# A two-block kernel on one core: filler matmuls in TensorE's waits, all PSUM banks open, and the pooled branch in another order

## The chip, the cores and the metric

The kernel runs on one core of one Trainium2 chip. The metric is the device time of one execution in microseconds (us). The core's engines run side by side: TensorE (PE, matrix products), VectorE (DVE), ScalarE (ACT, which also issues some DMAs), GpSimd (POOL), and SyncE (SP, here only DMAs). They meet through semaphores. All data is float32.

## The reference, cut to what matters

```python
def first_block(x, c, ...):            # x: 512 tokens x 1024
    shift1, scale1, gate1, shift2, scale2, gate2 = split(silu(c) @ w_ada + b_ada)
    a = rms(x, norm1_w) * (1 + scale1) + shift1
    x = x + gate1 * hybrid_mixer(a)    # SSD + dilated attention + pooling, summed, @ w_out
    a = rms(x, norm2_w) * (1 + scale2) + shift2
    return x + gate2 * (relu(a @ w_ff1) ** 2 @ w_ff2)

def second_block(x, c, ctx, c_ctx, ...):   # 512 latent and 256 context tokens, 4 layers
    for i, mixer in enumerate((window_gqa, mla, mlstm, window_gqa)):
        sh, sc, gt = split(silu(c) @ w_ada_i + b_ada_i)      # the same for c_ctx
        h = rms(x, g_pre_i) * (1 + sc) + sh                  # latent and context
        x = x + gt * rms(mixer(h), g_post_i)
    return x_lat
```

The pooled branch of the hybrid mixer takes `u = a @ w_in[u]` in four groups of 256 channels, subtracts from group g its causal mean over 2, 4, 8 or 16 tokens, mixes each group with a 256x256 matrix, scales, and gives `sigmoid(a @ w_in[g_pool]) * (mixed @ w_pool_out)` to the sum of the branches.

## The kernel before, in words

**Layout.** Activations lie feature-major: a tensor of 1024 features is 8 chunks of 128 partitions by the tokens. Each operand of a large product is split into a rounded part and a remainder (`a_hi`, `a_lo`; `w_hi`, `w_lo`), and `products` (L414 to L418) makes three matmuls of each pair of chunks. A tile of 128 outputs by 512 tokens over 8 chunks is 24 matmuls into one PSUM bank.

**Weights.** They arrive in 156 slots of 128x2048 in a ring of three. SP starts the DMA of a slot when the slot three earlier is used up, ACT writes `w_hi` (L411), POOL writes `w_lo` in four pieces (L402), and PE waits for `lo_ready`. A slot holds two full tiles. The order of the slots is fixed by `slot_plan` (L49).

**`dense`** (L421) is the stage that nearly all large products go through. It takes named weight sections, a function that gives a slot's tiles, and what ACT (`act_tile`), DVE (`dve_tile`) and ACT again (`act_last`) do to each finished tile. PE takes a bank only when the tile `ring` places back has been read out; `ring` is 4 where a slot has at most two tiles, else 6 or 8. In all stages ACT starts with a wait until every tile of the stages before has been read out (L497 ff.), DVE too. With `lead=2` the first two tiles run side by side, chunk by chunk, as the chunks of `a` come. `rhs_ready` holds what PE waits for before a chunk that another engine still has to write.

**Modulation.** The six and twelve vectors `silu(c) @ w_ada` are worked out on DVE: 72 slots are streamed in, and one slot is two instructions of 128x1024 (L765), or four from slot 24 on, where both conditioning vectors are needed. The slots are shared out over the tiles of some `dense` stages: in group form 8 in the setup, 8 in `z`, 8 in the SSD's output stage, 16 in `qkv0` and `qkv1` (8 each), 32 in the eight feed-forward stages (4 each). A slot's products stand on DVE ahead of the work on that tile.

**Order of the program.** First norm (L967), SSD branch (`z`, `dt`, `xbc`, then small stages of transposes, states and heads, L1140 to L1340), its norm (`rms_scale`, L827) and output; dilated attention (`qkv0` to `qkv3` with `HeadNorms` L1409 as side work, then the last norms alone, then `group_attention` L1475); output of it; the pooled branch (L2036); `out`; a norm (`pre_norm`, L866); four pairs of feed-forward stages `ff1_b`, `ff2_b` (L2163 to L2182). Then the second block: A0 (window attention, L1726), B (latent attention, `pair_attention`, L1578), C (mLSTM) and A3 (window attention again), each with its `pre_norm`, where PE sums squares into all rows with a matrix of ones (L913).

**The pooled branch before.** `u` runs through groups 0 to 3 (2-wide mean first); ACT copies each tile, and `pool_tile` on DVE takes the mean by doublings (L2069) and splits the result into `m_hi`, `m_lo` (group 3 needs the most instructions). `mix` waits for them and `scaled` (L2097) makes `x_hi`, `x_lo`. `gated` (L1342) then runs four turns of two gate tiles (`g_pool`, a product with `a`) and two output tiles (`pool_out`, a product with `x`). Its `dense` starts once all of `mix` is read out, since ACT's entry wait and the bank ring both ask for it.

**The attention stages.** `window_attention` issues the scores of pair p+1, transposes and value products of earlier pairs; `pair_attention` does the same with three banks of 512 a score. In B, `finish_both` (on DVE, L2375, L599, L600) multiplies a head pair's output with its gate over all 768 tokens when its last query block is done, and the output stage waits for that.

## Time and profile before

| | |
|---|---|
| median of 3 runs | 3040.9 us |
| lowest and highest | 3038.96, 3047.11 us |
| the profiled execution | 3038.86 us |
| its span in the trace | 3037.1 us |
| mean granted TensorE clock | 0.965 of full |
| PE busy | 2781.2 us (92%) |
| DVE busy | 1629.8 us (54%) |
| ACT busy | 1224.1 us (40%) |
| POOL busy | 955.4 us (31%) |

The span is what the instructions take on the device; the execution's own time has 1.8 us more around it. Busy PE time counts overlapping records once. Two records of one float32 matmul stand in the trace, one of each product matmul of `dense`. The granted clock of TensorE has two levels here, full (2.4 GHz, shown as 1.0) and half (1.2 GHz).

### The profile page before, as it was taken

How to read it: one execution, taken by the hardware profiler on the slowest of the kernel's cores; microseconds unless marked ns; L12 is line 12 of the kernel's file. 1: busy time of each engine (PE TensorE's matmuls, PEld its weight loads, DVE VectorE, ACT ScalarE, POOL GpSimd, SP SyncE). 2: the span in 40 equal slices, each digit the busy share in tenths (PEclk: the TensorE clock that was granted, in tenths of full speed). 3: DMA queues.
4: the chain of work that ended last, by engine and by line, in shares of the span. 5: the costliest groups of instructions: out<-in, count | busy, mean ns of one | idle time of the engine just before them, and what ended most of it. 6: DMA issues, size and time to landing. Idle time of an engine off the chain costs nothing.

```text
span 3037.1 us, 39956 instructions
## 1 busy us (share of the span) xinstructions
PE 2781.2 (92%) x16048; PEld 2289.2 (75%) x16048; DVE 1629.8 (54%) x3096; ACT 1224.1 (40%) x2113; POOL 955.4 (31%) x636
## 2 busy tenths in 40 slices
PE   5978989889899899989999989999899999889996
PEld 4746878678687788869876868677689998768785
DVE  6686394162832999960288341354490238551583
ACT  4334234543123222242278354543442326353582
POOL 4612475304453666633300213100233220113301
PEclk8989999999999999999999999999999999999998
DMA  8303562202323555521200221101122331122201
GB/s 322 123 28 146 189 219 104 98 1 84 125 96 126 194 193 182 194 112 69 95 10 2 84 83 56 42 1 49 61 85 69 140 131 51 56 83 102 72 2 70
DMA packets 52329, 300.07 MB, mean 99 GB/s; under 512 B 4592, under 2 KB 5936, under 8 KB 22320
## 3 DMA queue, kind: packets, MB, share of 16 engines
q1 hardware_dynamic: 22464, 163.59, 15.2%
q10 hardware_dynamic: 29680, 133.92, 11.7%
q8 instruction: 128, 2.10, 0.3%
q14 instruction: 57, 0.47, 0.0%
HBM read 271.25 MB, written 21.00 MB: 96 GB/s over the span
## 4 chain that ended last, share of the span: by engine, by line
PE 67%; DVE 14%; ACT 4%; issue 2%; DMA 0%; ACTq 0%; DVEq 0%
PE psum L416 17%; PE psum L417 17%; PE psum L418 17%; DVE ada_temp L765 4%; PE psum L1768 2%; PE psum L913 2%; PE psum L1610 2%; PE psum L3054 2%; PE psum L1633 2%; PE psum L1789 2%; DVE pair_row L1818 1%; PE psum L1778 1%; PE psum L1614 1%; PE psum L1622 1%; DVE pair_prob L1827 1%
## 5 line engine op out<-in xcount | busy, mean ns | idle before, releaser
L402 POOL TENSOR_TENSOR w_lo<-raw,w_hi 128x512 fp32r<-128x512 f32 x624 | 945.3, 1546 | 2039.9 <-ACT w_hi L411 2039.8
L416 PE MATMUL psum<-a_hi,w_hi 128*128 128x512 f32 (+2 forms) x1880 | 709.1, 377 | 71.9 <-DVE a_lo L922 20.6
L418 PE MATMUL psum<-a_hi,w_lo 128*128 128x512 f32 (+2 forms) x1880 | 698.7, 372 | 0.0
L417 PE MATMUL psum<-a_lo,w_hi 128*128 128x512 f32 (+2 forms) x1880 | 698.6, 372 | 0.0
L416 PEld LDWEIGHTS psum<-a_hi,w_hi 128*128 128x128 f32 (+1 forms) x1880 | 358.1, 190 | 147.4 <-issue 44.4
L765 DVE SCALAR_TENSOR_TENSOR ada_temp<-ada_ring,ada_rows 128x1024 f32<-128x1024 f32 x224 | 393.1, 1810 | 48.5 <-ACT ada_rows L725 21.3
L417 PEld LDWEIGHTS psum<-a_lo,w_hi 128*128 128x128 f32 (+1 forms) x1880 | 358.3, 191 | 64.0 <-issue 3.6
L418 PEld LDWEIGHTS psum<-a_hi,w_lo 128*128 128x128 f32 (+1 forms) x1880 | 357.0, 190 | 62.8
L411 ACT ACTIVATE w_hi<-raw 128x2048 fp32r<-128x2048 f32 x156 | 298.2, 1912 | 243.9 <-DMA raw<-stream 133.5
L416 PE MATMUL psum<-w_hi,a_hi 128*128 128x256 f32 x800 | 229.7, 287 | 1.1 <-POOL w_lo L402 0.6
L417 PE MATMUL psum<-w_lo,a_hi 128*128 128x256 f32 x800 | 226.3, 283 | 0.0
L418 PE MATMUL psum<-w_hi,a_lo 128*128 128x256 f32 x800 | 226.3, 283 | 0.0
L416 PEld LDWEIGHTS psum<-w_hi,a_hi 128*128 128x128 f32 x800 | 153.4, 192 | 3.4 <-issue 1.4
L417 PEld LDWEIGHTS psum<-w_lo,a_hi 128*128 128x128 f32 x800 | 153.5, 192 | 1.4 <-issue 1.4
L418 PEld LDWEIGHTS psum<-w_hi,a_lo 128*128 128x128 f32 x800 | 153.4, 192 | 0.0
L1818 DVE CUSTOM_DVE_ANT_0 pair_row<-psum,pair_mask,neg_sinks 128x512 f32<-128x512 f32 (+2 forms) x160 | 116.6, 747 | 37.7 <-PE psum L1768 24.8
L1846 ACT ACTIVATE pair_prob<-pair_row,pair_stat 128x513 f32<-128x513 f32 (+2 forms) x160 | 114.8, 719 | 42.3 <-DVE pair_stat L1818 24.8
L2308 DVE TENSOR_TENSOR square<-y 128x512 f32<-128x512 f32 (+1 forms) x56 | 33.3, 594 | 173.8 <-ACT y L2314 173.8
L1768 PE MATMUL psum<-gk,gq 64*128 64x128 f32 (+1 forms) x960 | 97.7, 338 | 17.3 <-DVE pair_stat L1818 15.5
L2314 ACT ACTIVATE y<-psum 128x512 f32<-128x512 f32 (+1 forms) x56 | 28.3, 506 | 199.2 <-PE psum L418 198.8
L416 PE MATMUL psum<-hid_hi,w_hi 128*128 128x512 f32 x256 | 99.8, 390 | 1.4 <-DVE hid_lo L600 1.4
L1768 PEld LDWEIGHTS psum<-gk,gq 64*128 64x128 f32 x960 | 72.0, 194 | 36.7 <-DVE pair_stat L1818 23.4
(397 smaller groups left out, 4633.3 us busy)
## 6 DMA issues: line engine op xcount, KB each, us to landing
raw<-stream SPq DMA_DIRECT2D x156, 1024.0 KB, 4.8
ada_ring<-ada ACTq DMA_DIRECT2D x72, 1024.0 KB, 5.7
xres<-x_in ACTq DMA_DIRECT2D x4, 3072.0 KB, 11.1
x_in<-xres ACTq DMA_DIRECT2D x3, 3072.0 KB, 10.8
gates<-gate_part ACTq DMA_DIRECT2D x8, 768.0 KB, 4.2
partner<-gq ACTq DMA_DIRECT2D x4, 1024.0 KB, 10.2
c_rows_m<-rows_m ACTq DMA_DIRECT2D x2, 1536.0 KB, 9.3
c_og<-gates ACTq DMA_DIRECT2D x4, 768.0 KB, 5.7
```

Source lines behind the costliest of these rows:

```text
L402: last = pool.tensor_tensor(k.w_lo[:, r, cols], k.raw[:, r, cols], k.w_hi[:, r, cols].bitcast(F32), ALU.subtract)
L411: act.activation(k.w_hi[:, r], k.raw[:, r], ACT.Copy).then_inc(k.hi_ready, 1)
L416: pe.matmul(out, lhs[0], rhs[0], start=start, stop=False)
L417: pe.matmul(out, lhs[0], rhs[1], start=False, stop=False)
L418: return pe.matmul(out, lhs[1], rhs[0], start=False, stop=stop)
L765: dve.scalar_tensor_tensor(self.temp[:, self.products % 2], self.ring[:, place, c], 1.0, self.used_rows[:, w], ALU.mult, ALU.mult, accum_o ...
L913: pe.matmul(k.psum[:, banks[n], 0:t1 - t0], k.cst("ones"), squares[:, i % 2, 0:t1 - t0], start=c == 0, stop=c == KC - 1).then_inc(summed.s ...
L1610: pe.matmul(score(u)[:, col:col + cols], q, keys, start=True, stop=False)
L1633: last = pe.matmul(value_bank(u), units[u]["pv"][j], prob_t[:, u % n_t, j * P:(j + 1) * P], start=j == 0, stop=j == n_blocks - 1)
L1768: last = pe.matmul(score(u)[:, col:col + cols], q, keys, start=True, stop=True)
L1818: dve.tensor_tensor_reduce(row[:, u % 4, 1:1 + w], score(u), mask[:, un["mask"]:un["mask"] + w], 1.0, un["sink"], ALU.add, ALU.min, stat[: ...
L1846: act.activation(prob[:, u % 4, 0:1 + width(u)], row[:, u % 4, 0:1 + width(u)], ACT.Exp, bias=stat[:, 0, u % 4:u % 4 + 1], scale=-1.0, acc ...
```

## The change

- **Fillers.** `keep_busy(pe, bank, n)` issues n float32 matmuls (a 128x128 matrix of ones by 256 constant columns) into a bank that nobody reads. They stand in PE's program ahead of a wait or behind one: in `z` ahead of chunk 4 (4) and chunk 6 (14); after `xbc` (11); in the SSD's small stages (2, 8, 5, 7); in `rms_scale` (5, it is called with two groups); around the last head norms (6 and 11); at the start of `ff1_0` (10) and `ff2_0` (4); in `pre_norm` of the second block ahead of the latent and the context sums (6 and 6; in A0 only the second); at the start of `Aq`, `Bin` and `Cqk` (5 each); in window attention behind the scores in turns 0 and 1 (5 each) and at its end (4); at the end of B's attention (11); in C ahead of the last head's first turn (20) and at its end (4).
- **Banks.** `ring` is now every bank a stage may use (8, or 6 where `n_banks=6`).
- **ScalarE's entry.** With `untaken=n`, ACT's wait at the start of a stage allows n tiles of the stages before to be still unread, and where the stage has no `act_tile` it doesn't wait at all. `ff1_1` to `ff1_3`, `ff2_b` and the pooled stages use `untaken=8`.
- **Pooled branch.** `u` and `mix` go through the groups from 3 to 0; a stage `g_pool0` (the gate tiles of turn 0, kept in `sig`, now four tiles) stands between them; then three turns each have the gates of the next turn and the output tiles of this one; `pool_out3` is last.
- **Modulation.** The dilated attention's group shrinks from 16 slots to 12 (`qkv1` 8 to 4), the feed-forward's grows from 32 to 36 (each `ff1_b` 4 to 3, each `ff2_b` 4 to 6).
- **B's gate product** is made in two parts: latent tokens after query block 3, context tokens after block 5.

```diff
-    slots("u", "w_in", full, R(u0, 1024))
-    slots("mix", "mix", (0, 1024), R(0, 256))
+    slots("u", "w_in", full, [x for g in (3, 2, 1, 0) for x in R(u0 + 256 * g, 256)])
     for c in range(4):
         slots(f"g_pool{c}", "w_in", full, R(g0 + 2048 + 256 * c, 256))
-        slots(f"pool_out{c}", "w_pool_out", full, R(256 * c, 256))
+        if c:
+            slots(f"pool_out{c - 1}", "w_pool_out", full, R(256 * c - 256, 256))
+        else:
+            slots("mix", "mix", (0, 1024), R(0, 256))
+    slots("pool_out3", "w_pool_out", full, R(768, 256))
...
+    def keep_busy(self, pe, bank, n):
+        for _ in range(n):
+            pe.matmul(bank[:, 0:256], self.cst("ones"), self.const[:, 0:256], start=True, stop=True)
...
-    ring = 4 if max(per) <= 2 else 6 if max(per) % 3 == 0 else 8
...
-    ring = min(ring, n_banks - k.odd_banks)
+    ring = n_banks - k.odd_banks
...
                     pe.wait_ge(free.sem, free.at(together - ring))
+                    k.keep_busy(pe, bank(0), fill)
                     for j in range(len(slot_tiles[0][1])):
+                        if lead_fill and j in lead_fill:
+                            pe.wait_ge(free.sem, free.at(together + 1 - ring))
+                            k.keep_busy(pe, bank(together), lead_fill[j])
...
                     pe.wait_ge(free.sem, free.at(t + 1 - ring))
+                    if t == 0:
+                        k.keep_busy(pe, bank(t), fill)
...
-        act.wait_ge(free.sem, free.at(0))
+        if act_tile is not None or untaken == 0:
+            act.wait_ge(free.sem, free.at(-untaken))
...
+    if fill_end:
+        @block.tensor
+        def _(pe):
+            pe.wait_ge(free.sem, free.at(1 - n_banks))
+            k.keep_busy(pe, bank(total), fill_end)
...
+            if c == 0 and fill[n]:
+                pe.wait_ge(k.tile_free.sem, k.tile_free.at(0))
+                k.keep_busy(pe, k.psum[:, next(b for b in (2, 3, 4) if b not in banks), :], fill[n])
             pe.wait_ge(sq.sem, sq.at(i + 1))
...
+        pe.wait_ge(masked.sem, masked.at(2 * n))
+        k.keep_busy(pe, k.psum[:, 0, :], 11)
...
             if p + 1 < n:
                 scores(p + 1)
+            if p < 2:
+                k.keep_busy(pe, k.psum[:, 7, :], 5)
             if p >= 3:
                 values(p - 3)
+        pe.wait_ge(masked.sem, masked.at(2 * n))
+        k.keep_busy(pe, k.psum[:, 0, :], 4)
...
-    ada = k.ada.group(16, B0 + 36864, B0 + 61440, rest + 20480, 3, new_rows=True)
+    ada = k.ada.group(12, B0 + 36864, B0 + 61440, rest + 20480, 3, new_rows=True)
...
+    pooled = k.free_of
+    sig = k.at("sig", B0 + 100352, [P, 4, S])
+    dense(k, block, ["g_pool0"], feature_major(a, KC, [(0, S)]), barrier=False, untaken=KC,
+          dve_tile=lambda dve, i, t, ps: dve.nop(),
+          act_tile=lambda act, i, t, ps: act.activation(sig[:, t, :], ps, ACT.Sigmoid))
...
+    k.rhs_ready = {(j, 2 * g + c): (k.tile_free.sem, pooled[2 * g + j])
                    for g in range(4) for c in range(2) for j in range(2)}
-    dense(k, block, ["mix"], mix_tiles, dve_tile=scaled, barrier=False)
+    dense(k, block, ["mix"], mix_tiles, dve_tile=scaled, barrier=False, untaken=KC)
...
+    def gate_ahead(act, i, t, ps):
+        if t >= 2:
+            act.wait_ge(k.staged.sem, staged + 4 * i + t)
+            return act.nop()
+        if i:
+            act.wait_ge(k.tile_free.sem, start + 4 * i - 1 + t)
+        return act.activation(sig[:, 2 * ((i + 1) % 2) + t, :], ps, ACT.Sigmoid)
...
+    k.rhs_ready = {(j, 2): (k.tile_free.sem, mixed_at[j]) for j in range(KC)}
+    dense(k, block, [f"{x_}" for c in range(3) for x_ in (f"g_pool{c + 1}", f"pool_out{c}")],
+          lambda s, hi, lo: feature_major(x if s else a, KC, [(0, S)])(s, hi, lo), turn_slots=2, act_tile=gate_ahead,
+          dve_tile=project, barrier=False, untaken=KC)
...
+    dense(k, block, ["pool_out3"], feature_major(x, KC, [(0, S)]), barrier=False, untaken=KC,
+          dve_tile=lambda dve, i, t, ps: add_chunk(dve, 6 + t, ps))
...
-    ada = k.ada.group(32, B0 + 57344, A0 + 40960, B0 + 81920, 3, new_rows=True)
+    ada = k.ada.group(36, B0 + 57344, A0 + 40960, B0 + 81920, 3, new_rows=True)
...
-              ada=ada.of(4), barrier=False)
+              ada=ada.of(3), barrier=False, untaken=KC if b else 0)
...
-        dense(k, block, [f"ff2_{b}"], feature_major(hid, KC, full), dve_tile=add_ff, ada=ada.of(4), barrier=False)
+        dense(k, block, [f"ff2_{b}"], feature_major(hid, KC, full), dve_tile=add_ff, ada=ada.of(6), barrier=False, fill=0 if b else 4, untaken=KC)
...
-        if b == 5:
-            pair["finish"] = finish_both(c)
+        if b in (3, 5):
+            pair["finish"] = finish_both(c, LAT if b == 3 else CTX)
...
+                if (h, c) == (H - 1, 0):
+                    k.keep_busy(pe, front(q), 20)
                 pe.wait_ge(normed.sem, normed.at(6 * h + 6))
```

**What it moves on ScalarE, pooled branch.** `u` is the copy of a tile of `u`, `sig` a gate tile, `w_hi` a weight slot's rounding, `x_in` the residual read back; the stage borders are the branches. Before:

```order
L2080 ACTIVATE u_6340<-psum 128x512
L496 UNCONDITIONAL_BRANCH
L411 ACTIVATE w_hi_51<-raw_49 128x2048
L2105 UNCONDITIONAL_BRANCH
L2139 DMA x_in_6339<-xT 128x8x512
L2140 DMA x_in_6339<-ctxT 128x8x256
L496 UNCONDITIONAL_BRANCH
L1356 ACTIVATE sig_6864<-psum 128x512
```

And of the change:

```order
L2126 ACTIVATE u_6373<-psum 128x512
L514 UNCONDITIONAL_BRANCH
L2133 ACTIVATE sig_6756<-psum 128x512
L421 ACTIVATE w_hi_51<-raw_49 128x2048
L2133 ACTIVATE sig_6756<-psum 128x512
L514 UNCONDITIONAL_BRANCH
L421 ACTIVATE w_hi_51<-raw_49 128x2048
L2157 UNCONDITIONAL_BRANCH
L2221 DMA x_in_6372<-xT 128x8x512
L2222 DMA x_in_6372<-ctxT 128x8x256
L514 UNCONDITIONAL_BRANCH
L2173 ACTIVATE sig_6756<-psum 128x512
```

The first two gate tiles and one more weight slot now stand between the last tile of `u` and the stage `mix`.

**What it moves on VectorE, feed-forward.** `ada_temp` are modulation products (a slot each, x4), `x_in` the sum of one `ff2` tile into the residual, `mod` the bias of the finished vectors. The first `ff2` stage before:

```order
L765 SCALAR_TENSOR_TENSOR ada_temp_63,mod_7_56<-ada_ring_7823,ada_rows_7824 128x1024 x4
L2177 SCALAR_TENSOR_TENSOR x_in_6339<-psum,mod_6_55,x_in_6339 128x512 x2
L765 SCALAR_TENSOR_TENSOR ada_temp_63,mod_7_56<-ada_ring_7823,ada_rows_7824 128x1024 x4
L2177 SCALAR_TENSOR_TENSOR x_in_6339<-psum,mod_6_55,x_in_6339 128x512 x3
L786 TENSOR_TENSOR mod_7_56<-mod_7_56,cols_53 128x16
```

And of the change:

```order
L790 SCALAR_TENSOR_TENSOR ada_temp_63,mod_7_56<-ada_ring_7862,ada_rows_7863 128x1024 x4
L2258 SCALAR_TENSOR_TENSOR x_in_6372<-psum,mod_6_55,x_in_6372 128x512
L790 SCALAR_TENSOR_TENSOR ada_temp_63,mod_7_56<-ada_ring_7862,ada_rows_7863 128x1024 x4
L2258 SCALAR_TENSOR_TENSOR x_in_6372<-psum,mod_6_55,x_in_6372 128x512 x3
L811 TENSOR_TENSOR mod_7_56<-mod_7_56,cols_53 128x24
```

These are the ends of the two stages: a whole `ff2` stage has four such blocks of modulation products before and six in the change, so that nearly every tile's sum stands behind one.

**What it adds on TensorE, SSD.** From the end of `xbc` to the transposes, the change:

```order
L356 MATMUL psum<-const_52 128x256 x11
L369 UNCONDITIONAL_BRANCH
L1169 UNCONDITIONAL_BRANCH
L356 MATMUL psum<-const_52 128x256 x2
L1174 MATMUL psum<-const_52,dt_rows_1436 128x16 x4
L356 MATMUL psum<-const_52 128x256 x8
L1179 MATMUL psum<-dt_2008,const_52 128x64
```

The rows of L356 are the fillers; before, the four transposes of `dt_rows` stood alone between the two stage borders.

## Rows read from the trace of the kernel before

**Rows 1.** The page: engines' busy time, and the chain that ended last.

```profile
PE 2781.2 (92%) x16048; PEld 2289.2 (75%) x16048; DVE 1629.8 (54%) x3096; ACT 1224.1 (40%) x2113; POOL 955.4 (31%) x636
...
PE 67%; DVE 14%; ACT 4%; issue 2%; DMA 0%; ACTq 0%; DVEq 0%
```

**Rows 2.** PE's waits: line, releaser, us in total, times, longest.

```profile
PE psum L913 <- ACT squares L897: 25.6, 7, 3.8
PE psum L416 <- DVE a_lo L922: 20.6, 9, 5.7
PE psum L416 <- DVE a_lo L1018: 20.4, 3, 11.9
...
PE psum L416 <- DVEq L366: 14.6, 5, 5.8
PE psum L416 <- POOL w_lo L402: 14.0, 6, 6.2
...
PE psum L849 <- ACT squares L840: 6.2, 2, 3.7
```

**Rows 3.** Timeline of PE: start us, us, instruction, [idle before, releaser]. C.

```profile
2525.31 4.17 PE L3054 MATMUL psum<-cv,c_decay 128*128 128x257 f32 x18 [0.92 <-DVE c_decay L3159]
```

**Rows 4.** Timeline of PE and of DVE in the z stage.

```profile
48.74 0.79 PE L416 MATMUL psum<-a_hi,w_hi 128*128 128x512 f32 x1 [6.45 <-DVE a_lo L1018]
...
50.32 0.69 DVE L1018 TENSOR_TENSOR a_lo<-psum,a_hi 128x512 fp32r<-128x512 f32 x1 [1.04 <-ACT psum L1039]
```

**Rows 5.** Timeline of PE after xbc, SSD.

```profile
168.01 0.61 PE L1143 MATMUL psum<-const,dt_rows 16*128 16x16 f32 x4 [6.23 <-ACTq L371]
...
174.98 7.44 PE L1166 MATMUL psum<-const,xbc 128*128 128x128 f32 x40 [1.43 <-ACTq L371]
```

**Rows 6.** Transposes in window attention, and a stretch's busy times and clock.

```profile
1552.04 1.09 PE L1778 MATMUL psum<-const,pair_prob 128*128 128x128 f32 x8
...
1540.00:1640.00 100.00, 97.95 (x1144) 81.20 (x1140) 85.60 (x254) 83.01 (x201) 0.00 (x0) 1.00 0.01 2
```

**Rows 7.** Timeline of PE: a head norm in qkv2, first scores of group attention.

```profile
484.63 1.22 PE L1447 MATMUL psum<-squares,const 128*128 128x512 f32 x1 [2.01 <-DVE qkv L1465]
...
606.67 1.65 PE L1495 MATMUL psum<-qkv 128*128 128x128 f32 x6 [6.63 <-DVEq L366]
```

**Rows 8.** Timeline of PE and of DVE in the pooled branch.

```profile
805.31 0.65 PE L416 MATMUL psum<-m_hi,w_hi 128*128 128x512 f32 x1 [4.32 <-DVE m_lo L600]
...
817.43 0.76 PE L416 MATMUL psum<-a_hi,w_hi 128*128 128x512 f32 x1 [8.20 <-DVE x_lo L600]
817.99 0.63 PE L417 MATMUL psum<-a_lo,w_hi 128*128 128x512 f32 x1
818.42 0.63 PE L418 MATMUL psum<-a_hi,w_lo 128*128 128x512 f32 x1
...
822.14 0.69 DVE L600 TENSOR_TENSOR x_lo<-mixed,x_hi 128x512 fp32r<-128x512 f32 x1
```

**Rows 9.** Feed-forward stretches: PE, PEld, DVE, ACT, POOL busy; last: L765 alone.

```profile
982.60:1326.30 343.70, 335.89 (x1468) 276.12 (x1467) 320.18 (x391) 76.69 (x64) 231.03 (x126) 1.00 0.51 185
1066.80:1153.40 86.60, 86.60 (x384) 71.71 (x383) 80.29 (x98) 19.57 (x16) 59.04 (x32) 1.00 0.54 193
...
982.60:1326.30 343.70, 232.70 (x256) 1.00 0.51 185
```

**Rows 10.** Timeline of PE: sums of squares in layer B's norm.

```profile
1751.96 10.83 PE L913 MATMUL psum<-squares,const 128*128 128x512 f32 x18 [3.62 <-ACT squares L897]
```

**Rows 11.** Timeline of PE and DVE: attention starts and ends.

```profile
1520.03 2.51 PE L1768 MATMUL psum<-gk,gq 64*128 64x128 f32 x16 [2.03 <-DVE pair_stat L1818]
...
2099.48 0.96 DVE L600 TENSOR_TENSOR b_lo<-mq,b_hi 128x768 fp32r<-128x768 f32 x1
...
2103.29 0.77 PE L416 MATMUL psum<-b_hi,w_hi 128*128 128x512 f32 x1 [5.85 <-DVEq L366]
...
2617.97 2.79 PE L3042 MATMUL psum<-const,c_og 128*128 128x128 f32 x12 [10.12 <-DVE c_og L3185]
```

More of the change, by code:

```diff
@@ L845, in _ @@
     def _(pe):
+        k.keep_busy(pe, k.psum[:, banks[0], :], 5)
         for c in range(n_chunks):
@@ L1933, in _ @@
                 act.wait_ge(ada.used, ada.used_at(ada.end))
-        dense(k, block, [f"qkv{j}"], tiles, act_tile=take, ada=ada.of(8) if j < 2 else None, barrier=j == 3,
+        dense(k, block, [f"qkv{j}"], tiles, act_tile=take, ada=ada.of((8, 4)[j]) if j < 2 else None, barrier=j == 3,
               n_banks=6, side=side)
@@ L2109, in _, with add_chunk, project @@
         residual_in(act)
-    gated(k, block, a, x, [f"{x_}{c}" for c in range(4) for x_ in ("g_pool", "pool_out")], acc, B0 + 26112,
-          out_parts, {(j, 2): (k.tile_free.sem, k.free_of[j]) for j in range(KC)})
+    mixed_at = [k.free_of[chunk_of(c)] for c in range(KC)]
+    start, staged = k.tile_free.base, k.staged.base
+    def gate_ahead(act, i, t, ps):
[5 more added lines that the diff above has]
+        return act.activation(sig[:, 2 * ((i + 1) % 2) + t, :], ps, ACT.Sigmoid)
+    def add_chunk(dve, c, ps):
+        s = sig[:, c % 4, :]
+        k.dve_chain(dve, dve.tensor_tensor(s, ps, s, ALU.mult))
+        k.dve_chain(dve, dve.tensor_tensor(acc[:, c, :], acc[:, c, :], s, ALU.add))
+        return split(k, dve, out_parts[0][:, c, :], out_parts[1][:, c, :], acc[:, c, :])
+    def project(dve, i, t, ps):
+        if t < 2:
+            dve.wait_ge(k.tile_free.sem, start + 4 * i + t)
+            return dve.nop()
+        return add_chunk(dve, 2 * i + t - 2, ps)
+    k.rhs_ready = {(j, 2): (k.tile_free.sem, mixed_at[j]) for j in range(KC)}
+    dense(k, block, [f"{x_}" for c in range(3) for x_ in (f"g_pool{c + 1}", f"pool_out{c}")],
+          lambda s, hi, lo: feature_major(x if s else a, KC, [(0, S)])(s, hi, lo), turn_slots=2, act_tile=gate_ahead,
+          dve_tile=project, barrier=False, untaken=KC)
+    ready = [k.free_of[c // 2 * 4 + 2 + c % 2] for c in range(6)]
+    dense(k, block, ["pool_out3"], feature_major(x, KC, [(0, S)]), barrier=False, untaken=KC,
+          dve_tile=lambda dve, i, t, ps: add_chunk(dve, 6 + t, ps))
+    return ready + k.free_of
 def first_block(k, block, first_ada):
@@ L2141, in residual_in @@
             .then_inc(k.sem_named("context_loaded").sem, 16)
-    pool_branch(k, block, a, acc, m, residual_in)
+    m_ready = pool_branch(k, block, a, acc, m, residual_in)
     @block.vector
@@ L2151, in add @@
         return dve.scalar_tensor_tensor(x[:, t, :], ps, k.mod1[:, 16 + t:17 + t], x[:, t, :], ALU.mult, ALU.add)
-    k.rhs_ready = {(c, 0): (k.tile_free.sem, k.free_of[c // 2 * 4 + 2 + c % 2]) for c in range(KC)}
+    k.rhs_ready = {(c, 0): (k.tile_free.sem, m_ready[c]) for c in range(KC)}
     dense(k, block, ["out"], feature_major(m, KC, full), dve_tile=add, barrier=False)
@@ L2600, in into @@
         return put
-    dense(k, block, ["Bin"], feature_major(a, KC, both), act_tile=into(raw, ACT.Copy), barrier=False, lead=2)
+    dense(k, block, ["Bin"], feature_major(a, KC, both), act_tile=into(raw, ACT.Copy), barrier=False, lead=2, fill=5)
     steps = LatentSteps(k, raw, low, R0 + 36864)
@@ L2664, in unit_of, with finish_both @@
                     mask=0, pv=[v[:, kb, h * P:(h + 1) * P] for kb in blocks])
-    def finish_both(c):
-        chunks = [finish_chunk(k, q, z, b2, h, 0, T2) for h in (2 * c, 2 * c + 1)]
+    def finish_both(c, part):
+        chunks = [finish_chunk(k, q, z, b2, h, *part) for h in (2 * c, 2 * c + 1)]
         def finish(dve):
```

48 lines of the change are left out of this document (29 added, 19 removed).

## The prediction

> **What bounds the kernel now.** I read the page first, then PE's waits, then the timeline around each wait. The page shows PE busy for 2781.2 us and holding 67% of the chain that ended last, DVE 14% [rows 1]. So PE is the bound nearly everywhere, and time can be won only where PE idles or runs at the half clock. Its waits [rows 2] are short and many: 25.6 us in seven waits for sums of squares (L913), 20.6 us for `a_lo` of a norm, 20.4 us for `a_lo` in `z` and before it, 14.6 us at stage borders, 14.0 us for `w_lo`. Behind most waits of over 2 us a stretch stands at the half clock.
>
> **Prices.** A product matmul of 128x512 takes 86.60 us / 384 = 0.226 us at full clock [rows 9] and 0.43 us at half (the step from 817.99 to 818.42) [rows 8]: 0.20 us lost each, some ten of them behind a wait. No filler stands in the old trace. Its nearest row is the float32 matmul of 257 columns at full clock: 18 records, two a matmul, in 4.17 us, 0.46 us each [rows 3]. I take 0.45 us, and twice that, 0.9 us, at the half clock. All 217 fillers thus cost 98 us of PE at full clock. A filler in a wait that is longer costs nothing; what reaches past the wait is lost.
>
> **The sum, against the profiled execution (3038.9 us; the median is 2.0 us above it).**
>
> 1. *`z`.* PE waits 6.45 us for chunk 4 at 48.74, and chunk 6 is ready at 50.32+0.69 = 51.0 [rows 4]. Chunks 4 and 5 alone keep PE past that. The four fillers ahead of chunk 4 hide; the 14 ahead of chunk 6 stand where nothing is waited for: 14x0.45 = 6.3 us. About 1 us of it comes back, since a later wait for `w_lo` [rows 2] shrinks. **+5** (bounds: +8, if they run partly at half clock; +2, if they give back the cold chunks 4 and 5).
> 2. *SSD.* Fillers of 11x0.45 = 5.0 in a wait of 6.23, 8 (3.6) in one of 3.81; 40 transposes take 7.44 us, 0.186 each [rows 5], against 1.09/8 = 0.136 at full clock [rows 6]: up to 2 us to win, of which the transposes' readers on ACT and DVE take part. **−1** (−3 to +2). The trace speaks of this: in 1540 to 1640 the clock stays at 1.00 with transposes among scores [rows 6]. The Trainium skill ("TensorE: Matmul & The Clock Gate", Part 4: PE-mode transpose) says that transposes don't count as activity for the full clock; by that rule this term would be 0.
> 3. *`rms_scale`.* 5 fillers (2.3 us) in each of two waits, 6.2 us together [rows 2]. The matmuls there are paced by ACT's squares. **0** (−1 to +1.5).
> 4. *`qkv2`.* DVE has 16 modulation products less in `qkv1` (29 us at the price of rows 9); the wait of 2.01 us at 484.63 for DVE [rows 7] and three cold matmuls go: **−2.6** (0 to −3). The waits for `w_lo` stay: `qkv0` keeps its slots.
> 5. *Start of group attention.* 6.63 us idle ahead of 606.67, then six transposes in 1.65 us [rows 7], twice the price of rows 6, and cold scores until about 618. With the clock held some 12 us of work at half speed win a third: **−4** (−5 to 0).
> 6. *Pooled branch.* `u` ends at 791.8. Then `mix` waits 4.32 us for `m_lo` and the gates 8.20 us for `x_lo`; together with 19 cold matmuls (19x0.20 = 3.8) [rows 8] that is 16.3 us. Now `g_pool0` (10.9 us) fills 791.8 to 802.7 while DVE ends the pooling at 805.3; `mix` follows it, gate 1 runs to about 819, and `pool_out0` starts as `x` comes (chunk 0 is the seventh that DVE makes, some 2 us before 822.8 [rows 8]). **−17** with the entry waits (−5, if `x` holds `pool_out0` up; −17.5).
> 7. *Norm before the feed-forward.* 10 fillers (4.5) in a wait of 5.7 us (the longest of its line) [rows 2], 12 cold matmuls: **−2.3**, counted in the next term.
> 8. *Feed-forward.* Here the change loads DVE: 4 slots more, 16 products. The products took 232.7 us for 128, 1.82 each; so +29 us on a DVE that was busy 320.2 of 343.7 us [rows 9]. In the middle pair DVE has 80.29 + 4x1.82 = 87.6 us against PE's 86.6: it becomes the bound. With its small waits it ends about 5 us late, less the 2.3 of term 7: **+3** (−7, if PE's early waits go and DVE keeps up; +10). The dear form of a product, beside POOL, is what the row's mean mixes in. The Trainium skill ("SBUF — State Buffer", Who interferes with whom) says that such an instruction is locked out by POOL wholly, not slowed; if each of the new products meets POOL's work, the trace's mean would be too low and this term near its upper bound, 3016 us in all.
> 9. *Norms of the second block.* A0's one wait: −1.7. Layers 1 to 3 each have a wait of 3.62 ahead of the latent sums, whose 18 records take 10.83 us [rows 10], the same ahead of the context sums, and 2.9 with 7 to 9 cold matmuls (1.6 us) behind. 6 fillers take 2.7 us of 3.6. Warm sums take 8 us at DVE's pace: −2.7; the cold products −1.6: 4 us a layer. **−13.7** (−17 to −6, if the sums are bound by DVE after all).
> 10. *Window attention.* The waits after the first scores are 2.03 us and 1.9 or 3.1 us [rows 11]; five fillers are 2.25 us at full, 4.5 at half clock. **+1.5** each in A0 and A3, **+3** (−3 to +5).
> 11. *End of B.* The wait of 5.85 us holds six DVE instructions over 768 tokens, 0.96 the longest [rows 11]; with the context third alone about 2.4 us are left, but 11 fillers take 5.0, from an earlier start. The 14 cold matmuls (2.8 us) go. **−3.5** (−4 to −1).
> 12. *End of C.* 10.12 us idle, then transposes in 2.79 us [rows 11], 12 at 0.23: **−1.2** (0 to −2).
>
> Sum: 5 −1 +0 −2.6 −4 −17 +3 −13.7 +3 −3.5 −1.2 = **−32.0**. 3038.9 − 32.0 = 3006.9; against the median, **3009 us**.
>
> ScalarE's entry without the wait costs nothing beyond the places above: elsewhere ACT has 60% idle [rows 1]. Eight banks instead of four let PE run ahead of DVE by more tiles; that shifts waits, it doesn't add work. Of the DMAs none is new; weights come in the new order at the same count.
>
> **The rivals.**
>
> - *The fillers run at the half clock and reach past their waits* (slower). Where the clock has fallen before they start, or they don't hold it, each costs 0.9 us. Waits hold about 3.6 us, four fillers; the groups of 5 to 14 overshoot. All 217 would be 195 us, in waits of about 110 us: +85, plus no clock won back, against −17 of the pool and −2.6: about +65, 3106 us. It decides from a mean price of some 0.65 us: 217x0.65 = 141, 31 past the waits, as much as the rest wins. For it: PE has just idled or is about to where several groups start. Against it: most stand directly behind full-clock matmuls. A partial form, +12 to +30, is likelier than the whole.
> - *DVE doesn't become the bound in the feed-forward.* The first stage has DVE idle until 982.6 and its products run at 1.2 us without POOL beside them. Term 8 is −7 and the norms reach their end of the range: −32 −10 −4 = −46, about 2995 us. For: 23.5 us of DVE are idle there. Against: the middle pair has 6.3 us idle for 7.3 us of new work [rows 9].
> - *The pooled branch turns its wait into another.* `x_lo` is made by the same chain on DVE; `pool_out0` would wait for it and term 6 is −5: 3021 us. For: DVE isn't a microsecond faster. Against: 10.9 us of gates lie between.
> - *The change doesn't hold the clock* (the fillers cost nothing, win nothing): terms 2, 5, 9 and 11 fall to −7 together: 3024 us.
>
> **How the numbers follow.** About 0.3% (9 us) is what a measurement of this kernel can tell from no change. Chances: the sum as it stands 0.50; feed-forward not bound by DVE 0.18; pooled wait moved 0.10; clock not held 0.12 (half of it ends within 9 us); fillers at half clock 0.10 (half in the partial form, within 9 us or just beyond, half slower). So faster by over 0.3% is 0.85, within 0.3% 0.09, slower 0.06. The range from 2990 to 3027 us holds the forecast's own spread (15 us either way from the bounds of terms 1, 8 and 9), the second and third rival and most of the fourth; it leaves out the slow end and the tail below.
>
> **What would show it.** Right: the wait for chunk 4 in `z` is shorter and a run of 14 fillers of 6 us stands between chunks 5 and 6; no wait of over 2 us after `u`, `g_pool0`'s end at 803 and the pooled branch's `out` ends 17 us earlier relative to `u`; the stretch of the four feed-forward pairs with DVE over 97% busy and PE waiting for `hid_lo`; the latent sums of layers 1 to 3 in about 8 us; no half-clock matmul behind norms and attention. Wrong: fillers with steps of 0.9 us; the half clock behind them all the same; PE's waits in the feed-forward near zero.

## The result, and the profile after

The change takes 3021.2 us (3020.4 to 3022.4, 4 runs) against 3042.8 us (3039.0 to 3047.1, 4 runs) for the kernel before on the same chips: a ratio of 0.9930, 95% interval 0.9917 to 0.9942. It is faster by 0.7%, 21.6 us. The forecast was 3009 us, range 2990 to 3027. The profiled execution's span is 3018.7 us, against 3037.1 us.

The page of the kernel after, first section, then the chain that ended last (answers to [rows 1]):

```profile
PE 2842.6 (94%) x16482; PEld 2348.1 (78%) x16482; DVE 1612.0 (53%) x3120; ACT 1224.5 (41%) x2113; POOL 944.8 (31%) x636
...
PE 50%; DVE 16%; ACT 3%; issue 2%; POOL 1%; DMA 1%; PEldq 0%; DVEq 0%; ACTq 0%; PEld 0%
```

PE is busy 61 us more, since the fillers count as busy (they are 103.8 us; the rest fell by 42 us, as more of it ran at the full clock). Its mean granted clock rose from 0.965 to 0.986. Busy time of PE is no longer a measure of work. PE's waits after (line, releaser, total, times, longest; [rows 2]):

```profile
PE psum L426 <- DVE a_lo L1047: 17.4, 3, 11.2
PE psum L426 <- POOL w_lo L412: 14.5, 9, 3.4
...
PE psum L426 <- DVE a_lo L951: 10.1, 11, 2.0
...
PE psum L942 <- ACT squares L923: 9.0, 8, 2.1
...
PE psum L356 <- ACTq L381: 5.9, 3, 2.7
...
PE psum L426 <- DVE x_lo L625: 4.5, 2, 3.6
```

Most of what vanished here is covered by fillers, not gone. What counts is when each stage's own work starts. I took those starts from PE's timelines of both kernels:

| stretch | before, us | after, us | gained (−) | forecast |
|---|---|---|---|---|
| `z`, `dt`, `xbc` to the dt transposes | 136.3 | 141.6 | +5.3 | +5 |
| SSD, its norm and output | 182.8 | 181.5 | −1.3 | −1 |
| `qkv0` to `qkv3` | 235.6 | 231.4 | −4.2 | −2.6 |
| last head norms and group attention | 94.9 | 96.6 | +1.8 | −4 |
| attention output and pooled branch | 225.9 | 216.4 | −9.5 | −17 |
| `out`, norm, feed-forward, A0's sums | 435.7 | 438.8 | +3.1 | +3 and −1.7 |
| A0 from its sums on, B to its attention | 588.6 | 585.5 | −3.1 | −4 and +1.5 |
| B's attention, output and C's sums | 268.2 | 260.2 | −8.0 | −7.5 |
| C's products, attention and output, A3's sums | 517.7 | 512.6 | −5.1 | −5.2 |
| A3's products and attention | 253.6 | 256.7 | +3.1 | +1.5 |

The rest of the 18.4 us is rounding and the first and last few microseconds. (Where a stretch holds parts of two terms, both forecasts stand in it.)

The "before" column comes from one of the fastest executions of that kernel (3038.9 us; its medians beside the experiments were 3043.9 to 3046.6 us). Other executions differ from it in the SSD above all: experiment 11, with the same code there, took 187.9 us in place of 182.8; 2.5 us of that lie in the norm behind it (`rms_scale`), where more of the sums ran at the half clock. PE's timeline of the kernel before, then of experiment 11:

```profile
258.33 5.40 PE L849 MATMUL psum<-squares,const 128*128 128x512 f32 x8 [3.71 <-ACT squares L840]
...
261.66 6.47 PE L849 MATMUL psum<-squares,const 128*128 128x512 f32 x8 [3.62 <-ACT squares L840]
```

From its first sum to the product behind it that norm takes 12.3, 12.4 and 14.9 us in the three traces without fillers, and 10.7 us in all eleven with them. So the table shows what the fillers win there against a fast execution, which is the least.

### The profile page after: what moved, and what is told of

Same layout as the page of the kernel before. It is cut to its first block, busy times and chain, and to the rows that moved or that the text cites. A ratio compares the mean times of both kernels' runs of the same rounds, so it can differ in the third digit from the quotient of the medians.

```text
span 3018.7 us, 40836 instructions
## 1 busy us (share of the span) xinstructions
PE 2842.6 (94%) x16482; PEld 2348.1 (78%) x16482; DVE 1612.0 (53%) x3120; ACT 1224.5 (41%) x2113; POOL 944.8 (31%) x636
## 4 chain that ended last, share of the span: by engine, by line
PE 50%; DVE 16%; ACT 3%; issue 2%; POOL 1%; DMA 1%; PEldq 0%; DVEq 0%; ACTq 0%; PEld 0%
PE psum L426 12%; PE psum L428 12%; PE psum L427 12%; DVE ada_temp L790 5%; PE psum L1804 2%; PE psum L3137 2%; PE psum L1644 2%; PE psum L1667 2%; PE psum L1825 1%; DVE pair_row L1858 1%; PE psum L1814 1%; DVE a_lo L951 1%; DVE h L965 1%; DVE y L2419 1%; PE psum L1648 1%
## 5 line engine op out<-in xcount | busy, mean ns | idle before, releaser
L412 POOL TENSOR_TENSOR w_lo<-raw,w_hi 128x512 fp32r<-128x512 f32 x624 | 934.8, 1529 | 2032.8 <-ACT w_hi L421 2032.8
L421 ACT ACTIVATE w_hi<-raw 128x2048 fp32r<-128x2048 f32 x156 | 298.4, 1913 | 274.9 <-DVE ada_temp L790 122.5
L790 DVE SCALAR_TENSOR_TENSOR ada_temp<-ada_ring,ada_rows 128x1024 f32<-128x1024 f32 x224 | 375.2, 1729 | 46.0 <-DVEq L1396 16.0
L356 PE MATMUL psum<-const 128*128 128x256 f32 x434 | 103.8, 392 | 10.6 <-ACTq L381 5.9
L356 PEld LDWEIGHTS psum<-const 128*128 128x128 f32 x434 | 83.5, 196 | 27.6 <-issue 14.5
```

Source lines behind the costliest of these rows:

```text
L356: pe.matmul(bank[:, 0:256], self.cst("ones"), self.const[:, 0:256], start=True, stop=True)
L412: last = pool.tensor_tensor(k.w_lo[:, r, cols], k.raw[:, r, cols], k.w_hi[:, r, cols].bitcast(F32), ALU.subtract)
L421: act.activation(k.w_hi[:, r], k.raw[:, r], ACT.Copy).then_inc(k.hi_ready, 1)
L790: dve.scalar_tensor_tensor(self.temp[:, self.products % 2], self.ring[:, place, c], 1.0, self.used_rows[:, w], ALU.mult, ALU.mult, accum_o ...
```

## The experiments

Twelve kernels, each with its own profile. "The change" stands at 3021.2 us. Two warnings for the reading. The runs of one kernel span 1 to 13 us, and the kernel before, run again beside the experiments, had medians from 3043.9 to 3046.6 us. And some stages vary between kernels whose code there is the same: A0's window attention took from 161.1 to 164.6 us with its fillers in, the pooled branch from 212.8 to 216.5 us, `z` 139.6 or 141.6 us, the feed-forward with A0's sums from 382.2 to 385.1 us. So differences under 3 us are read from the stage that was altered, not from the total.

**1. No fillers.**

```diff
-        for _ in range(n):
+        for _ in range(0):
```

> The change with every filler left out (no matmul is issued by keep_busy; the waits ahead of them stay). Theory A, fillers are worth having on balance: they win the clock in the norms of the second block (13 us there), at the start of the feed-forward (2.4) and at the end of B and of C (some 4), and lose 4.4 us in z and some 5 at the starts of window and group attention: without them 3030 to 3037 us, with half-clock matmuls again behind each norm. Rival, the gain of the change comes from the pooled branch, the banks and the shorter finish in B alone: 3021 us or less.

Measured: 3033.2 us, ratio 0.9969 (0.9956 to 0.9981) to before. The fillers are worth 12 us (8.4 us between the two profiles). They win 4.7 us from A0's attention output to B's attention, 4.7 and 3.0 us in the stretches of C's and of A3's sums, 1.9 at the end of C; they lose 5 us in `z`, 2 us at the last head norms and 3.4 us in A3's attention. Theory A holds.

**2. `z` without its fillers.** `lead_fill={4: 4, 6: 14}` becomes `lead_fill={}`.

> The change without the 4 and 14 fillers of the z stage alone. Theory A, the 14 stand where nothing is waited for and delay everything behind them: z ends 4 to 5 us earlier, the whole is 3016 to 3017 us. Rival, the fillers there keep a clock that is worth as much, or the time comes back at a wait for w_lo or for DVE in the SSD branch: 3020 to 3022 us.

Measured: 3021.6 us, 0.9931 (0.9916 to 0.9946). The rival. PE's timeline of the change shows the fillers close to their price. The two lines are one run of 28 records (two a filler), cut by the views at 55 us; from its start to the next product at 59.28 the 14 fillers take 5.85 us, 0.42 each:

```profile
53.43 1.89 PE L356 MATMUL psum<-const 128*128 128x256 f32 x8
54.72 4.91 PE L356 MATMUL psum<-const 128*128 128x256 f32 x22
```

Without them `z` is 4.8 us shorter, and the stages stay 4 us early up to the start of the feed-forward, at 952.2 in place of 956.0. There 2.9 us are lost up to the end of A0's sums (385.1 us in place of 382.2), and 2.9 more in A0's attention. Both stages vary by as much between kernels with the same code there. Experiment 3 starts the feed-forward 11 us earlier than the change and loses 0.2 us in it, so it isn't shown that the DVE-bound feed-forward took the gain back; where it went stays open.

**3. `pool_out` takes `x` in the order in which it is made.** PE adds up the chunks of `x` in the order 6, 7, 4, 5, 2, 3, 0, 1.

```diff
+    def x_tiles(hi, lo):
+        return [(cut, [pairs[chunk_of(j)] for j in range(KC)])
+                for cut, pairs in feature_major(x, KC, [(0, S)])(1, hi, lo)]
-    k.rhs_ready = {(j, 2): (k.tile_free.sem, mixed_at[j]) for j in range(KC)}
+    k.rhs_ready = {(j, 2): (k.tile_free.sem, mixed_at[chunk_of(j)]) for j in range(KC)}
```

> The change with the two tiles of every pool_out product taking the chunks of x in the order in which DVE makes them (6, 7, 4, 5, 2, 3, 0, 1) in place of 0 to 7. Theory A, the pooled branch gained 9 us and not 17 since pool_out0 waits for chunk 0, the seventh made, and then runs 14 matmuls at the half clock: the wait of 3.6 and 0.8 us shrinks below 1 us, the cold matmuls go, 3014 to 3016 us. Rival, x is late as a whole, so that the wait only moves to chunk 1, or the time comes back behind it: 3019 to 3022 us.

Measured: 3013.4 us, 0.9902 (0.9887 to 0.9917): 7.8 us less than the change. Theory A. PE's timeline of the change, then of this kernel:

```profile
829.92 0.47 PE L426 MATMUL psum<-x_hi,w_hi 128*128 128x512 f32 x1 [3.62 <-DVE x_lo L625]
...
831.67 0.80 PE L426 MATMUL psum<-x_hi,w_hi 128*128 128x512 f32 x1 [0.83 <-DVE x_lo L625]
832.26 0.63 PE L427 MATMUL psum<-x_lo,w_hi 128*128 128x512 f32 x1
```

```profile
821.94 0.39 PE L426 MATMUL psum<-x_hi,w_hi 128*128 128x512 f32 x1
```

The change waits 3.62 and 0.83 us and then runs 14 matmuls at the half clock; this kernel has one wait for `x_lo`, of 0.7 us, keeps its clock, and its branch takes 208.0 us in place of 216.4.

**4. The modulation slots as before** (16 and 32).

```diff
-    ada = k.ada.group(12, B0 + 36864, B0 + 61440, rest + 20480, 3, new_rows=True)
+    ada = k.ada.group(16, B0 + 36864, B0 + 61440, rest + 20480, 3, new_rows=True)
-    ada = k.ada.group(36, B0 + 57344, A0 + 40960, B0 + 81920, 3, new_rows=True)
+    ada = k.ada.group(32, B0 + 57344, A0 + 40960, B0 + 81920, 3, new_rows=True)
```

(and 8 in `qkv1`, 4 in every `ff1_b` and `ff2_b`).

> The change with the modulation slots shared out as before: 16 in the dilated attention, 32 in the feed-forward (4 in each stage). Theory A, the 16 added products make DVE end the feed-forward 7 us behind PE: that tail goes, qkv takes 2 to 4 us more, 3016 to 3019 us. Rival, DVE in the feed-forward is late anyway (waits and weights, not the number of products), and qkv loses its 4 us: 3021 to 3025 us.

Measured: 3015.3 us (3012.2 to 3020.6), 0.9911 (0.9893 to 0.9928): 5.9 us less than the change. The chain of waits of the change at the end of the feed-forward (start, us, what):

```profile
1300.00 6.14 DVE ada_temp L790 x7
...
1308.95 5.04 DVE ada_temp L790 x7
...
1315.70 8.23 DVE ada_temp L790 x8
1323.93 0.67 DVE x_in L2258
...
1325.31 3.32 PE psum L942 x4
```

PE made its last `ff2` product at 1318.6, and the last three tiles of `x` stand on DVE behind modulation products until 1323.9. DVE of experiment 4 there:

```profile
1311.06 1.40 DVE L2258 SCALAR_TENSOR_TENSOR x_in<-psum,mod,x_in 128x512 f32<-128x512 f32 x2
1317.06 0.75 DVE L2258 SCALAR_TENSOR_TENSOR x_in<-psum,mod,x_in 128x512 f32<-128x512 f32 x1 [4.60 <-PE psum L428]
```

Its products are done at 1311.1 and DVE waits 4.60 us for PE. Feed-forward and A0's sums take 375.9 us, in the change 382.2. In the `qkv` stages and the head norms the four slots cost 4.5 us more, of which group attention gives 2.3 back.

**5. Three edits at once** (2, 3 and 4).

> Three edits to the change at once: z without its fillers, pool_out in the order in which x is made, modulation slots shared out as before (16 and 32). Theory A, what is won ahead of the feed-forward was lost in it as long as DVE set its end; with DVE relieved the three add up: 4 + 7 + 5 us, 3004 to 3008 us. Rival, they overlap (all were paid out of one slack): 3011 to 3014 us.

Measured: 3011.1 us, 0.9887 (0.9872 to 0.9902). The rival's number, but its reason (one slack that all were paid from) isn't shown. Feed-forward and sums (376.9), the pooled branch (208.0) and `z` (136.7) are as short as in the single edits; the `qkv` stages take 235.2 us in place of 231.4, as long as before, and the wait of 2.0 us for DVE in `qkv2` [rows 7] is back: with 16 slots in `qkv0` and `qkv1` DVE is late there. That price is already in the 5.9 us of experiment 4. What is missing from the sum stands in stages that no edit touched: A0's attention takes 164.1 us (change 161.1), and from B's attention to C's sums it is 261.9 us (260.2). Why stays open.

**6. 36 slots shared 4 and 5.** `ada.of(3)` and `ada.of(6)` in the feed-forward become `ada.of(4)` and `ada.of(5)`.

> The change with its 36 modulation slots in the feed-forward shared 4 to each ff1 and 5 to each ff2 stage in place of 3 and 6. Theory A, DVE idles some 20 us in the ff1 stages (six waits of 3.29 us for a tile) and lacks them behind ff2: with an even share that idle time is used and the tail behind the last product shrinks from 7 us to 2 or less, 3015 to 3018 us. Rival, the number of products alone sets DVE's end: 3020 to 3022 us.

Measured: 3021.8 us, 0.9922 (0.9906 to 0.9939). The rival in the total. My tail theory was right on the tail (A0's sums end 16.2 us behind PE's last product, as in experiment 4, in place of 19.7) and wrong on the gain: PE took 366.5 us for the feed-forward in place of 362.6. Its longest wait there is one of 7.0 us for `w_lo`, where the change has four of 5.1 us together. With 36 slots the time is the same either way; the share only chooses where PE waits.

**7. The ring as before.**

```diff
-    ring = n_banks - k.odd_banks
+    ring = min(4 if max(per) <= 2 else 6 if max(per) % 3 == 0 else 8, n_banks - k.odd_banks)
```

> The change with the ring of banks as before (4 where a slot has at most two tiles, 6 or 8 else). Theory A, eight open banks let PE run ahead of DVE in ff1_0 and in the gates, which the feed-forward's DVE-bound end hides: 3020 to 3025 us, with waits for hid_lo or free banks in the feed-forward. Rival, with only four banks PE is held to a DVE that stands behind five to six modulation slots in ff2, and the whole is 3030 us or more. If the banks do nothing, no wait differs.

Measured: 3023.0 us, 0.9924 (0.9909 to 0.9938). Theory A: the pooled branch takes 216.6 us, as in the change; feed-forward and sums 383.4.

**8. The pooled branch as before** (slots, `pool_branch` and `gated` of the kernel before, all else of the change).

> The change with the pooled branch as before (groups 0 to 3, mix directly behind u, gates in their own turn). Theory A, the new order is worth the 9.4 us seen between the two traces, and the DVE-bound feed-forward doesn't hide it, since DVE starts there when the norm ends: 3028 to 3032 us. Rival, part of it is swallowed in the feed-forward: 3022 to 3026 us. By my forecast's 17 us it would be 3038 us.

Measured: 3020.1 us, 0.9916 (0.9902 to 0.9931). Neither theory: it is no slower at all. Its branch takes 214.5 us, with one wait, PE's timeline:

```profile
804.41 0.80 PE L423 MATMUL psum<-m_hi,w_hi 128*128 128x512 f32 x1 [4.33 <-DVE m_lo L622]
```

The wait of 8.20 us for `x_lo` [rows 8] is gone, though the order is the old one. So I asked what took it away. But this kernel takes the chunks of `x` in the order in which they are made, and the change doesn't. The like comparison is with experiment 3, which does too: 208.0 us for its branch against 214.5, and 3013.4 us (0.9902) against 3020.1 (0.9916). So the new order is worth some 6.5 us in the branch once `x` is taken as it is made.

**9. Fillers in other places.** In `z` `lead_fill={4: 13}`; no fillers around the last head norms; none in turns 0 and 1 of window attention.

> The change with three groups of fillers altered: in z 13 ahead of chunk 4 and none ahead of chunk 6; none around the last head norms (6 and 11 before); none in turns 0 and 1 of window attention (5 each). Theory A: the 13 stand inside the wait of 6.4 us and give chunks 4 to 7 the full clock, so z to the dt transposes takes 133 to 135 us (before 136.3, change 141.6); the last norms go back to 13.2 us and group attention stays at 81 us, since DVE paces it; A0's and A3's attention lose the 2 and 3.3 us that the fillers cost. In all 3010 to 3014 us if the DVE-bound feed-forward passes it on. Rival: what is won ahead of the feed-forward is lost in it, as when z was bare: 3016 to 3019 us.

Measured: 3015.5 us (3011.7 to 3020.9), 0.9902 (0.9887 to 0.9917). The total is between the two; the stages say more. A0's attention takes 160.3 us and A3's 126.9 (change: 161.1 and 129.6; the bare kernel before 160.8 and 125.9): the fillers there only cost. Head norms: 14.1 (15.3), group attention as before: the same. `z` is 136.5 us and not 134. PE's timeline of this kernel:

```profile
43.11 5.78 PE L356 MATMUL psum<-const 128*128 128x256 f32 x26
48.54 0.58 PE L426 MATMUL psum<-a_hi,w_hi 128*128 128x512 f32 x1
48.96 0.40 PE L427 MATMUL psum<-a_lo,w_hi 128*128 128x512 f32 x1
...
78.32 0.50 PE L426 MATMUL psum<-a_hi,w_hi 128*128 128x512 f32 x1 [2.21 <-POOL w_lo L412]
```

The fillers do what they should: chunks 4 to 7 run at the full clock. A wait of 2.21 us for `w_lo`, 0.81 in the kernel before, takes part of that back: `z` is bound by the weights there.

**10. All these edits** (3, 4 and 9 together).

> The edits of the fillers' places, of the order in which pool_out takes x and of the modulation split (16 and 32 slots) together. Theory A, with PE and not DVE at the end of the feed-forward each stage's gain reaches the end: 3011 us of the three-edit kernel less 3 (z), 1 to 2 (norms), 4 to 5 (window attention): 3001 to 3004 us. Rival, modulation in qkv1 meets POOL's weights and gives back what z gains: 3006 us or more.

Measured: 3003.3 us (2998.8 to 3011.9), 0.9864 (0.9846 to 0.9882): the fastest of all, 18 us below the change, and inside theory A's numbers. The stages altered are as short as alone: pooled branch 207.9, feed-forward and sums 376.3, window attention 160.7 and 127.3; only `z`, at 138.2 us, is not: its wait for `w_lo` is 3.10 us here.

**11. The kernel before with the ring open, and nothing else.**

```diff
-    ring = min(ring, n_banks - k.odd_banks)
+    ring = n_banks - k.odd_banks
```

> The kernel before with nothing changed but the ring: every bank open in place of 4, 6 or 8. Theory A, the open banks alone let the gates of turn 0 start behind mix while DVE makes x, as the new order does by other means: the pooled branch takes 9 to 11 us less (215 to 217 us from the first output tile of the attention to the last pool_out, 225.9 before), the feed-forward's first waits go too, 3030 to 3034 us. Rival, ScalarE's wait at the stage's entry holds the gates up all the same and it takes both, banks and entry: 3040 us or more.

Measured: 3036.7 us (7 runs) against 3045.4, 0.9965 (0.9954 to 0.9977): 8.6 us from one line between the medians (7 to 14 us by the interval). Theory A on the mechanism; the total lies between the two theories' numbers. PE's timeline: the last of `mix`, then the gates at once.

```profile
812.57 0.63 PE L417 MATMUL psum<-m_lo,w_hi 128*128 128x512 f32 x1
813.00 0.59 PE L418 MATMUL psum<-m_hi,w_lo 128*128 128x512 f32 x1
813.42 0.39 PE L416 MATMUL psum<-a_hi,w_hi 128*128 128x512 f32 x1
```

With four banks PE had to wait until DVE had read out four tiles of `mix` (`x_lo` was named as the releaser [rows 8], but of the bank, not of an operand). With eight it runs the gates, 11 us of work, while DVE makes `x`. The branch takes 215.4 us, before 225.9. The two profiled executions are only 1.7 us apart, mostly since this one lost 5.1 us in the SSD, whose code is the same.

**12. ScalarE's old wait at every entry.**

```diff
-        if act_tile is not None or untaken == 0:
-            act.wait_ge(free.sem, free.at(-untaken))
+        act.wait_ge(free.sem, free.at(0))
```

> The change with ScalarE's old wait at every stage's entry (until all tiles of the stages before are read out). Theory A, the new entry buys nothing that the open banks do not: the pooled branch stays at 213 to 217 us, the feed-forward within 3 us of the change's, 3019 to 3024 us. Rival, with the wait ScalarE's weight slots behind it come late: PE waits for w_lo of over 3 us at the borders of the pooled and feed-forward stages, 3028 us or more.

Measured: 3018.2 us, 0.9913 (0.9897 to 0.9930). Theory A, if anything faster. The pooled branch takes 211.4 us, under my bounds: PE waits 1.38 and 0.83 us for `x_lo` and its clock stays. Why DVE is 2 us earlier there wasn't traced further; POOL's pieces fall elsewhere.

## Why the prediction was right, and where it was not

The direction, the range and the kind of gain were right, the size was not: 18.4 us between the profiled executions in place of 32.0, or 3021.2 us in place of 3009 by the medians. Point by point:

- **Term 6, the pooled branch, is the step that failed by size**: −17 forecast, −9.5 measured. Two things in it. I took chunk 0 of `x` to be ready some 2 us before 822.8, by DVE's times in the old trace. But DVE ended the pooling at 810.4, not 805.3, which is 16.9 us behind the end of `u` in place of 13.5 (`u` itself ended 1.7 us later), and made `x_lo` late:

```profile
809.82 0.69 DVE L625 TENSOR_TENSOR m_lo<-u,m_hi 128x512 fp32r<-128x512 f32 x1
...
828.14 1.63 DVE L625 TENSOR_TENSOR x_lo<-mixed,x_hi 128x512 fp32r<-128x512 f32 x1
```

  The same instruction takes 0.69 or 1.63 us, the second with a slot's `w_lo` pieces on POOL beside it. With the groups turned round chunk 0 is made seventh and used first. My third rival named this wait and priced it too high; experiment 3 takes it away and gets 7.8 us. And I put the gain down to the new order. Experiments 8 and 11 show that the order as built (groups turned round, `x` still taken from chunk 0) buys nothing once the banks are open, and that the line I dismissed with "that shifts waits, it doesn't add work" gives the same gain by itself; experiment 7 shows that the order does it with four banks too. Each is enough, so neither alone is missed. The sum also read the 8.20 us ahead of the gates as a wait for `x_lo`, an operand that a gate product doesn't have. What the order can give, 6.5 us more, comes only with experiment 3's edit.

- **Term 5, group attention, had the wrong sign**: −4 forecast, +1.8 measured. The fillers are ahead of the norms' sums, but behind the stage's border, which itself takes 2.72 of the 3.85 us:

```profile
589.08 4.26 PE L356 MATMUL psum<-const 128*128 128x256 f32 x12 [2.72 <-ACTq L381]
...
608.76 1.44 PE L1529 MATMUL psum<-qkv 128*128 128x128 f32 x6 [1.89 <-DVEq L376]
```

  They ran at 0.71 us each, and the sums start at 593.2, 2.9 us later than before, though `qkv3` ended at the same time. The 11 behind the norms do speed up the first scores (1.44 us for 1.65 [rows 7]), and still group attention takes 81.3 us against 81.7: the waits for DVE between its scores are as long as before (3.8 us in six), so DVE paces it. Such a stage had no clock to win. The size of the loss is less sure than its sign: five other traces with the same fillers there have 95.1 or 95.2 us for the stretch, 0.2 or 0.3 above the kernel before.

- **Term 1** holds (`z` +5.3 for +5). **Terms 2 and 3** hold in sum (−1.3 for −1), with the parts exchanged: the SSD up to its norm and from it on took 170.8 us for 170.4, and the norm, forecast at 0, won 1.7 us, beyond its bound. In this trace the SSD's transposes behind fillers are at the full-clock price, 5.53/40 = 0.138 us:

```profile
179.86 5.53 PE L1198 MATMUL psum<-const,xbc 128*128 128x128 f32 x40 [1.45 <-ACTq L381]
...
179.00:186.00 7.00, 5.53 (x40) 4.22 (x40) 5.61 (x12) 0.37 (x2) 0.00 (x0) 1.00 0.00 0
```

  (second line: that stretch's busy times, the clock 1.00). That isn't so each time. With the same fillers ahead, experiments 2, 4, 5 and 7 took 6.33 to 6.60 us for these 40: the clock fell after three to seven of them, and it came back while only transposes ran. The kernel before, where they started cold, shows the rise too. Its trace at 178 and at 181, then experiment 4's at 180 and at 183:

```profile
178.00:180.80 2.80, 2.80 (x16) 2.80 (x15) 2.12 (x5) 0.00 (x0) 0.00 (x0) 0.50 0.00 0
181.00:182.40 1.40, 1.40 (x14) 1.18 (x11) 1.34 (x4) 0.00 (x0) 0.00 (x0) 1.00 0.00 0
...
180.00:182.50 2.50, 2.50 (x14) 2.50 (x13) 2.08 (x5) 0.00 (x0) 0.00 (x0) 0.50 0.00 0
183.00:185.00 2.00, 2.00 (x18) 1.70 (x16) 1.96 (x5) 0.00 (x0) 0.00 (x0) 1.00 0.00 0
```

  The rule of the Trainium skill weighed there ("TensorE: Matmul & The Clock Gate", Part 4: PE-mode transpose), that transposes don't engage the full clock, isn't borne out: the granted clock rose from 0.50 to 1.00 with nothing but transposes on PE.

- **Term 4**: −4.2 for −2.6, inside its idea: DVE was relieved in `qkv1`.

- **Terms 7 and 8, the feed-forward**: the number held (+3.1 for +3), partly by luck. DVE does set the end, but by the place of its work and not by its load: the 16 added products were to cost DVE 29 us and cost 9.8 (242.5 us for 144 in place of 232.7 for 128), and DVE was busy for 327.4 of 362.6 us, 90% and not over 97%. PE's own part took 362.6 us for 361.9; what grew is the tail from PE's last product to the end of A0's sums, 19.7 us for 17.1, where six slots a stage stand ahead of the last tiles' sums. Two details differ too. `ff1_0` starts no earlier behind the norm, since its wait is for `a_lo`; only the 12 cold matmuls went. And PE waits less for `hid_lo`, as I had written (2.2 us in two waits), than at the borders for `w_lo` (5.1 us in four, the longest 1.6): ScalarE stands in its own queue behind DVE, since it may load a modulation slot only when one is used up, and the next weights are behind that load. The page's group of `w_hi` shows it, 122.5 us of such waits where there were 64.6:

```profile
L421 ACT ACTIVATE w_hi<-raw 128x2048 fp32r<-128x2048 f32 x156 | 298.4, 1913 | 274.9 <-DVE ada_temp L790 122.5
```

  The added products didn't raise the price of one: the median of all of them (below the middle number of the three, in ns) fell from 2248 to 1643, presumably as fewer ran beside POOL; that wasn't counted.

```profile
L790 DVE SCALAR_TENSOR_TENSOR ada_temp<-ada_ring,ada_rows x224: 1207/1643/2315, 58.3 to 1321.6; 128x1024 f32<-128x1024 f32 x112
```

  So the upper bound by the rule of the port lock (the Trainium skill, "SBUF — State Buffer", Who interferes with whom) was not reached.

- **Term 9, the norms**: −9.6 in place of −13.7 (A0 0.2 behind its sums, B 3.1, C 2.6 beside 2.5 for the matmuls of B's output, A3 3.7). The latent sums take 8.31 us for 10.83 [rows 10], as forecast, and A0 won next to nothing, since its sums wait for DVE's tail (from the end of its latent to the end of its context sums, inside the stretch above, 8.4 us for 9.3). B's norm:

```profile
1747.26 8.31 PE L942 MATMUL psum<-squares,const 128*128 128x512 f32 x16 [0.94 <-ACT squares L923]
...
1776.46 0.51 PE L426 MATMUL psum<-a_hi,w_hi 128*128 128x512 f32 x1 [1.93 <-DVE a_lo L951]
```

  The wait behind the norm, for `a_lo`, is still 1.9 of 2.9 us; the fillers cover a wait, they don't end it.

- **Term 10**: +3.9 for +3. A3's first five fillers follow a wait of 3.06 us and run at the half clock, 0.88 us each, the second five at 0.49:

```profile
2828.01 2.50 PE L1804 MATMUL psum<-gk,gq 64*128 64x128 f32 x16 [3.06 <-DVE pair_stat L1858]
2830.44 4.42 PE L356 MATMUL psum<-const 128*128 128x256 f32 x10
2834.79 1.37 PE L1804 MATMUL psum<-gk,gq 64*128 64x128 f32 x16
2836.09 2.43 PE L356 MATMUL psum<-const 128*128 128x256 f32 x10
```

  This is the first rival, true here and in part at the head norms (0.71 us each) and not in general: all 217 fillers took 103.8 us, 0.48 each, where it needed 0.65.

- **Terms 11 and 12**: −5.4 for −3.5 and −1.8 for −1.2. In B the shorter finish gives most of it: experiment 1, without fillers, keeps 2.5 of the 2.9 us ahead of `Bo`.

So the 21.6 us are, in round numbers from experiments 1, 11 and 4: fillers 12, open banks 9, B's finish 2 to 3, less 4 to 6 for the moved modulation slots (by the stages they win 4.5 us up to the head norms, give 2.3 of it back in group attention and cost 6.3 in the feed-forward; by the totals the move costs 5.9). These overlap and aren't a sum to the microsecond (they come to 17 to 20): taken out of the change, the open banks are missed by 1.8 us (experiment 7), which is within the noise. The pooled branch's order, as built, and ScalarE's new entry show no gain of their own.

## What to carry to other kernels

- In these traces a filler paid where the wait ahead of PE's next work was longer than the fillers, began where they stand, and was followed by work that PE itself paces. (That the six at the head norms would pay ahead of the stage's border, and not behind it, is argued; no run moved them.) Measure from one stage's real work to the next; PE's busy time and its list of waits both look better with every useless filler.
- When a wait names the operand's writer, ask whether it is for the operand or for the bank that the same engine has to read out. Opening the ring was one line and gave by itself as much as the whole change won in the pooled branch.
- Moving an engine's work into another stage can make it the bound at that stage's end, though the engine isn't full: look at what stands ahead of the stage's last results. What was won ahead of the feed-forward did pass through it (experiment 3).
- A consumer should take its parts in the order in which they are made. Here a reordering showed its worth, 6.5 us, only once that was so.
- One trace is one execution. Compare a stage's length over every trace in which its code is the same before a difference of 1 or 2 us is called an effect.
